# Conv front of a two-layer decoder trunk: zero fills issued early and apart, bias row added by VectorE, own replica buffers, first loads re-ordered

## The chip, the cores and the metric

The kernel runs on one core of one Trainium2 chip. The metric is the device time of one execution in microseconds (us). A run measures the kernel before and the changed kernel on the same chip; the time given of the kernel before is the median of three runs.

## What is computed

A decoder trunk of two layers over 512 tokens of width 1024, all in float32. Layer 0 is a Conformer convolution module and a mixture of experts, layer 1 is a sliding-window attention and a mixture of experts. The change is in the convolution module, in the residual sums, and in two transfers that serve the first mixture of experts.

```python
def conformer_conv(x, w1, b1, dw, dwb, g, bn, w2, b2):
    h = x @ w1 + b1                                  # (512, 2048)
    a, gate = jnp.split(h, 2, axis=-1)
    h = a * jax.nn.sigmoid(gate)
    h = lax.conv_general_dilated(                    # causal, 31 taps, each of 1024 channels alone
        h, dw[:, None, :].astype(h.dtype), window_strides=(1,),
        padding=[(CONV_WIDTH - 1, 0)], dimension_numbers=('NWC', 'WIO', 'NWC'),
        feature_group_count=D_MODEL) + dwb
    h = jax.nn.silu(layer_norm(h, g, bn))
    return h @ w2 + b2

def deepnorm(x, sub, g, b):
    return layer_norm(DEEPNORM_ALPHA * x + sub, g, b)

# layer 0: x = deepnorm(x, conformer_conv(x, ...), ...); x = deepnorm(x, grouped_moe(x, ...), ...)
# layer 1: x = deepnorm(x, swa_sink_attention(x, ...), ...); x = deepnorm(x, grouped_moe(x, ...), ...)
```

The mixture of experts sends each token to two of 16 experts. The kernel puts the tokens into a table in HBM, `xs_dram`, which has places for 512 tokens of each expert and must hold zeros where no token stands.

## The kernel before

Every engine has a program of its own, written by hand, and the engines meet at semaphores only. The names that matter here are those of the convolution front, the first 290 us.

**Input.** ScalarE (ACT) issues the loads of x in four tiles of 128 tokens (L1212), then the small parameter rows (`prm`), the convolution weights `dw_r` of 31 rows by 1024 columns (L1217), the positions, and eight small pieces of the convolution weights in another layout (`dw_a`, L1223). SyncE (SP) issues at the same time the ten loads of the first weight matrix (`conv_in`, L385; pieces 0 and 1 are one column tile of 128 channels, the others two) and two of the second (L393). TensorE (PE) transposes x (L475), VectorE (DVE) copies the result to `xT` (L823).

**Eight column tiles.** For each tile c of 128 channels TensorE makes the product for `a` and `gate` (L508); after tile 0 come some transposes of parameters (L490 to L496). ACT makes the sigmoid (L1253), and VectorE the gated product `glu(c)` into `hpad` (L841). The 31 taps of tiles 0 to 3 are done by VectorE, one instruction each (`taps(c, glus)`, L849 to L862); the table `glus` says before which tap a `glu` of a later tile stands. Tiles 4 to 7 are done by TensorE (L522) as 32 products of 32 output channels each with weights `wdw`, which GpSimd (POOL) builds in one instruction (L1496). These products read `shifted(c)`: 16 pieces of `hpad`, shifted by 0 to 3 columns, which SP copies from SBUF to SBUF with 16 DMAs a tile (`replicate(c)`, L415). The copies of tiles 4, 5 and 6 go to ring slots 1, 2 and 3, those of tile 7 to slot 1 again, and wait for TensorE to be through with tile 4 (`s_pec`). ACT moves each result out of PSUM (L1260).

**Residual.** The layer norm that follows needs `ALPHA * x + b2`. POOL makes it in place in `x_sb`, two instructions for each of four tiles (L1491, L1492), once the row `resrow` and the other rows are there (`s_rows`); VectorE adds the product of the second matrix (L900). In layer 1 POOL does the same (`residual(t)`, L1598 and L1599), and VectorE adds at L1142.

**Zero fill.** `clear_rows(i)` (L1246) writes zeros over one half of `xs_dram`, 16 MB in one DMA that ACT issues. Half 0 is issued behind the row loads in `later_loads`, half 1 after the four results of L1260. The first scatter of tokens (L1530, POOL) waits for both.

**Then.** Normalisation, second matrix (L550), router and scatter, four token tiles in a row; after that the experts, whose weights go through a ring of eight buffers. SP issues the first five of these weight loads when TensorE has done tile 7 (`s_pec` at 4).

Of the kernel before, what the change touches and what calls it, by code (L numbers as in the profile page):

```python
# [24 lines left out]
ALU = mybir.AluOpType  # L25
# [3 lines left out]
P = 128  # L29
# [50 lines left out]
def trunk(nc, x_in, positions, conv_w1, conv_b1, conv_dw, conv_dwb, conv_ln_g, conv_ln_b,  # L80
# [12 lines left out]
    with ExitStack() as ctx:  # L93
# [3 lines left out]
        def sem(name):  # L97
            return ctx.enter_context(nc.semaphore(name))
# [141 lines left out]
        s_xa = sem("s_xa")  # L240
# [119 lines left out]
        def shifted(c):  # L360

            slot_of = (1, 2, 3, 1)[c - DVE_TILES]
            return wring[:, slot_of, 0:SHIFTS * REPW].rearrange("p (g n) -> p g n", g=SHIFTS)
# [16 lines left out]
        def _(sp):  # L380
# [7 lines left out]
            conv_in(0, 1)  # L388
            conv_in(1, 1)
# [20 lines left out]
            def replicate(c):  # L410

                sp.wait_ge(s_glu, c + 1)
                for s in range(SHIFTS):
                    for q in range(SHIFTS):
                        sp.dma_start(shifted(c)[s * GRP:(s + 1) * GRP, q, :],  # L415
                                     hpad[q * GRP:(q + 1) * GRP, c, s:s + REPW]).then_inc(s_rep[c - DVE_TILES], 16)

            replicate(4)
            replicate(5)
            sp.wait_ge(s_g1, KD)  # L420
            replicate(6)
            sp.wait_ge(s_pec, 1)
            replicate(7)
# [44 lines left out]
        def _(pe):  # L468
# [18 lines left out]
            def parameters():  # L487

                pe.wait_ge(s_small, 16 * 6)
                pe.transpose(ps[:, 5, 0:NPRM], prm[:, :], ident[0:NPRM, 0:NPRM])  # L490
                for c in range(DVE_TILES):
                    pe.transpose(ps[:, 4, 32 * c:32 * c + CW], dw_r[:, c * P:(c + 1) * P], ident[0:CW, 0:CW])
                pe.wait_ge(s_dwload, 16 * ROUNDS)
                pe.transpose(ps[:, 5, P:2 * P], dw_a.rearrange("p s c -> p (s c)"), ident[:, :])
                pe.wait_ge(s_rope, 1)
                pe.transpose(ps[:, 5, 64:64 + T], pos_f[:, :], ident[0:T, 0:T]).then_inc(s_prT, 1)  # L496
# [20 lines left out]
            for c in range(DVE_TILES, KD):  # L517
                pe.wait_ge(s_glu, c + 1)
                pe.wait_ge(s_rep[c - DVE_TILES], 16 * SHIFTS * SHIFTS)
                for r in range(ROUNDS):  # L520
                    for q in range(SHIFTS):
                        last = pe.matmul(ps[q * GRP:(q + 1) * GRP, 2 * (c % 4), :],  # L522
                                         wdw[:, r, SHIFTS * (c - DVE_TILES) + q, :],
                                         shifted(c)[:, q, SHIFTS * r:SHIFTS * r + S],
                                         start=(r == 0), stop=(r == ROUNDS - 1))
                last.then_inc(s_pec, 1)
# [280 lines left out]
        def _(dve):  # L807
# [18 lines left out]

            dve.wait_ge(s_prT, 1)
# [38 lines left out]
            taps(1, {4: 2, 22: 3})  # L866
            taps(2, {7: 4, 26: 5})
            taps(3, {10: 6, 28: 7})
# [28 lines left out]
            def add_product(t, bank, signal, count):  # L897

                for h in range(2):
                    ins = dve.tensor_tensor(x_sb[:, t, h * 512:(h + 1) * 512], x_sb[:, t, h * 512:(h + 1) * 512],  # L900
                                            ps[:, bank + h, :], ALU.add)
                ins.then_inc(signal, 1)
                dve.wait_ge(signal, count)
# [77 lines left out]
            dve.wait_ge(s_rows, 16 * 8)  # L981
# [5 lines left out]
            for t in range(T):  # L987
                if t >= 2:
                    places(0, t - 2, 7)
                dve.wait_ge(s_C, t + 1)  # L990
                dve.wait_ge(s_xa, t + 1)
                add_product(t, 4, s_cadd, t + 1)
                norm_x(t, n, 0, 0)
                n += 1
                if t + 2 < T:
                    norm_conv(t + 2, n)
                    n += 1
                if t >= 1:
                    route(0, t - 1)
# [109 lines left out]
            def take(u, n):  # L1109
# [28 lines left out]
                elif kind in ("W0", "W1"):  # L1138
# [3 lines left out]
                    dve.tensor_tensor(half_x, half_x, ps[:, bank, :], ALU.add).then_inc(bank_read[bank - 5], 1)  # L1142
# [61 lines left out]
        def _(act):  # L1204
# [12 lines left out]
            act.dma_start(dw_r[:, :], conv_dw[0]).then_inc(s_small, 16)  # L1217
# [3 lines left out]
            for r in range(ROUNDS):  # L1221
# [3 lines left out]
                              ).then_inc(s_dwload, 16)  # L1225

# [4 lines left out]
            def later_loads():  # L1231
# [4 lines left out]
                act.dma_start(resrow, conv_b2[0].partition_broadcast(P)).then_inc(s_rows, 16)  # L1236
# [12 lines left out]
            for c in range(KD):  # L1249
# [5 lines left out]
                if c == 0:  # L1255
                    later_loads()

# [5 lines left out]
            clear_rows(1)  # L1263
# [183 lines left out]
        def _(pool):  # L1447
# [20 lines left out]
            pool.wait_ge(s_small, 16 * 6)  # L1468
# [18 lines left out]

            pool.wait_ge(s_x0T, T)
            pool.wait_ge(s_rows, 16 * 8)
            for t in range(T):  # L1490
                own(pool.tensor_scalar(x_sb[:, t, :], x_sb[:, t, :], ALPHA, None, ALU.mult))  # L1491
                pool.tensor_tensor(x_sb[:, t, :], x_sb[:, t, :], resrow, ALU.add).then_inc(s_xa, 1)  # L1492
# [101 lines left out]
            pool.wait_ge(s_rows1, 16 * 5)  # L1594
            def residual(t):
                full(pool, ("Xa", t))
                full(pool, ("Xb", t))
                own(pool.tensor_scalar(x_sb[:, t, :], x_sb[:, t, :], ALPHA, None, ALU.mult))  # L1598
# [41 lines left out]
```

## Time and profile before

| what | value |
|---|---|
| median of 3 runs | 1178.7 us (1175.54 to 1180.32) |
| the profiled execution, its own time | 1174.66 us |
| its span (first to last instruction) | 1173.0 us |
| mean granted TensorE clock | 0.901 of full speed |
| TensorE matmul busy | 952.7 us, 81% |
| VectorE busy | 454.5 us, 39% |
| GpSimd busy | 220.9 us, 19% |
| ScalarE busy | 169.4 us, 14% |
| DMA, mean over the span | 267 GB/s |

The table is an average over stages with different limits, so it says little on a change to one stage. The times below are read on the scale of the span; what lies around the span is 1.66 us.

### The profile page before, as it was taken

The page shows a single profiled execution, that of the slowest core. Times are in us where ns is not written, and L with a number is a line of the kernel's source. Part 1 is how long each engine was busy: PE and PEld are TensorE (multiplying, and loading weights), DVE is VectorE, ACT ScalarE, POOL GpSimd, SP SyncE. Part 2 cuts the span into 40 slices and gives each one's busy share as a digit, 9 for nine tenths or more (in the row PEclk, how much of TensorE's full clock was granted, in tenths as well). Part 3 has the DMA queues.
Part 4 walks back from the last instruction along what each step waited for, and adds up shares of the span by engine and source line. Part 5 has one row for each costly group of instructions (what it writes and reads, how often), then busy time and mean ns, then how long its engine had stood idle before and what let it go on. Part 6 is the DMA issues. An engine that isn't in the chain of part 4 may idle for free.

```text
span 1173.0 us, 13864 instructions
## 1 busy us (share of the span) xinstructions
PE 952.7 (81%) x5241; PEld 499.1 (43%) x5241; DVE 454.5 (39%) x925; ACT 169.4 (14%) x376; POOL 220.9 (19%) x314
## 2 busy tenths in 40 slices
PE   6999969983999698999379899878459977999930
PEld 3444324542555354554134454434235534555510
DVE  1799913553111011111586548564511101111126
ACT  0000021311000000001113332432020000000110
POOL 1094000024211111100431002021240212020022
PEclk8999989985999899999589999978679978999975
DMA  8994349964999999999640003201859999999932
GB/s 252 387 409 157 87 152 414 402 226 170 345 389 403 373 390 384 382 408 411 214 180 1 1 1 144 72 1 68 322 201 392 387 372 391 388 383 395 398 127 107
DMA packets 74301, 313.40 MB, mean 267 GB/s; under 512 B 8797, under 2 KB 19209, under 8 KB 57704
## 3 DMA queue, kind: packets, MB, share of 16 engines
q1 hardware_dynamic: 36752, 228.83, 51.1%
q10 hardware_dynamic: 27352, 55.35, 12.6%
q0 software_dynamic: 10112, 28.06, 6.9%
q8 instruction: 56, 0.92, 0.3%
q14 instruction: 29, 0.24, 0.1%
HBM read 252.48 MB, written 55.31 MB: 262 GB/s over the span
## 4 chain that ended last, share of the span: by engine, by line
PE 58%; DMA 18%; DVE 15%; issue 4%; ACT 2%; POOL 2%; SPq 1%; POOLq 0%; ACTq 0%; DVEq 0%
PE ps L605 20%; PE ps L615 10%; DMA wring<-in_moe_w_gate_dram 8%; DVE arena L859 7%; PE ps L711 7%; PE ps L550 5%; PE ps L730 5%; DMA wring<-in_moe_w_up_dram 3%; PE ps L508 3%; DMA arena<-in_moe_w_up_dram 2%; DMA wring<-in_conv_w_dram 1%; PE ps L756 1%; PE ps L768 1%; DMA xs_dram<-x_sb,place_i 1%; PE ps L782 1%
## 5 line engine op out<-in xcount | busy, mean ns | idle before, releaser
L605 PE MATMUL ps<-wring,arena 128*64 128x256 f32 x2016 | 246.6, 403 | 55.3 <-DVE arena L1011 28.2
L605 PEld LDWEIGHTS ps<-wring,arena 128*64 128x64 f32 x2016 | 152.0, 146 | 149.6 <-issue 56.4
L1536 POOL DMA_DIRECT2D arena<-xs_dram x172 | 91.4, 536 | 357.0 <-DVE arena L1011 336.1
L615 PE MATMUL ps<-wring,arena 128*64 128x512 f32 x560 | 126.7, 594 | 6.2 <-DVE arena L1046 5.7
L508 PE MATMUL ps<-arena,wring 128*128 128x512 f32 x256 | 113.0, 604 | 4.2 <-DMA wring<-in_conv_w_dram 4.2
L1032 DVE COPY arena<-ps 128x256 f32<-128x256 f32 x32 | 13.6, 424 | 251.3 <-PE ps L648 251.3
L859 DVE SCALAR_TENSOR_TENSOR arena<-arena,dwT 128x512 f32<-128x512 f32 x116 | 96.1, 901 | 0.0
L711 PE MATMUL ps<-wring,arena 128*128 128x512 f32 x192 | 86.3, 605 | 3.5 <-ACT arena L1384 2.7
L605 PE MATMUL ps<-arena 128*64 128x256 f32 x736 | 83.2, 380 | 0.8 <-DMA arena<-in_moe_w_up_dram 0.7
L508 PEld LDWEIGHTS ps<-arena,wring 128*128 128x128 f32 x256 | 49.5, 194 | 66.3 <-issue 66.3
L1522 POOL TENSOR_TENSOR rstd<-vareps,half 128x1 f32<-128x1 f32 x20 | 25.7, 1287 | 271.6 <-DVE vareps L875 265.9
L615 PEld LDWEIGHTS ps<-wring,arena 128*64 128x64 f32 x560 | 39.4, 137 | 71.6 <-issue 60.5
L605 PEld LDWEIGHTS ps<-arena 128*64 128x64 f32 x736 | 52.1, 137 | 32.5 <-issue 6.0
L550 PE MATMUL ps<-wring,arena 128*128 128x512 f32 x128 | 62.5, 647 | 1.9 <-ACT arena L1273 1.3
L730 PE MATMUL ps<-wring,arena 128*128 128x512 f32 x128 | 60.2, 626 | 0.0
L1011 DVE STREAM_TRANSPOSE arena<-arena 128x512 f32<-128x512 f32 x43 | 47.5, 1105 | 30.3 <-DMA arena<-xs_dram 23.4
L711 PEld LDWEIGHTS ps<-wring,arena 128*128 128x128 f32 x192 | 36.5, 194 | 46.7 <-issue 45.6
L1320 ACT ACTIVATE arena<-ps 128x512 f32<-128x512 f32 x32 | 19.1, 597 | 227.3 <-PE ps L615 227.3
L1026 DVE TENSOR_TENSOR arena<-arena,ps 128x256 f32<-128x256 f32 x32 | 13.5, 421 | 89.2 <-PE ps L605 89.2
L550 PEld LDWEIGHTS ps<-wring,arena 128*128 128x128 f32 x128 | 26.2, 210 | 33.5 <-issue 31.8
L1044 DVE TENSOR_TENSOR arena<-arena,ps 128x256 f32<-128x256 f32 x11 | 4.6, 421 | 90.0 <-PE ps L605 90.0
L730 PEld LDWEIGHTS ps<-wring,arena 128*128 128x128 f32 x128 | 25.3, 203 | 30.3 <-issue 30.3
(189 smaller groups left out, 884.6 us busy)
## 6 DMA issues: line engine op xcount, KB each, us to landing
wring<-in_moe_w_gate_dram SPq DMA_DIRECT2D x24, 2048.0 KB, 25.1
wring<-in_moe_w_up_dram SPq DMA_DIRECT2D x24, 2048.0 KB, 19.7
wring<-in_moe_w_down_dram SPq DMA_DIRECT2D x24, 2048.0 KB, 20.2
xs_dram<-zero ACTq DMA_DIRECT2D x2, 16384.0 KB, 65.1
arena<-in_moe_w_up_dram SPq DMA_DIRECT2D x8, 2048.0 KB, 27.9
arena<-in_moe_w_down_dram SPq DMA_DIRECT2D x8, 2048.0 KB, 20.3
arena<-in_moe_w_gate_dram SPq DMA_DIRECT2D x8, 2048.0 KB, 25.7
arena<-xs_dram POOLq DMA_DIRECT2D x172, 64.0 KB, 7.1
```

What stands on the lines that cost most here:

```text
L508: last = pe.matmul(ps[:, 2 * (c % 4) + h, :], w[:, k, h, (c % 2) * P:(c % 2) * P + P], xT[:, k, :], start=(k == 0), stop=(k == KD - 1))
L550: last = pe.matmul(ps[:, 4 + h, :], hc[t % 2][:, c, :], slot(4 + c // 4, 4)[:, c % 4, h * 512:(h + 1) * 512], start=(c == 0), stop=(c == K ...
L605: mm = pe.matmul(ps[h * CAP:(h + 1) * CAP, bank, 0:256], act[:, k, :], w[:, k, h * 256:(h + 1) * 256], start=(k == 0), stop=(k == KD - 1))
L615: mm = pe.matmul(ps[h * CAP:(h + 1) * CAP, bank, :], act[:, j % 2, (j // 2) * CAP:(j // 2 + 1) * CAP], w[:, j, h * 512:(h + 1) * 512], sta ...
L711: last = pe.matmul(ps[:, bank, :], xTt[:, k, :], slot(at, KD)[:, k, :], start=(k == 0), stop=(k == KD - 1))
L730: last = pe.matmul(ps[:, bank, :], oT[t % 2][:, k, :], slot(3 + h, KD)[:, k, :], start=(k == 0), stop=(k == KD - 1))
L859: dve.scalar_tensor_tensor(out=acc, in0=hpad[:, c, k:k + S], scalar=dwT[:, c, k:k + 1], in1=acc, op0=ALU.mult, op1=ALU.add).then_inc(s_tap, 1)
L1011: return dve.transpose(xgT[i].rearrange("p k (h c) -> p h k c", h=2), xg[i].rearrange("p h (c k) -> p h k c", k=KD))
L1032: dve.tensor_copy(hT[b].rearrange("p a b -> p (a b)"), ps[:, 3, 0:256]).then_inc(s_hTc, 1)
L1320: act.activation(ysb[b], ps[:, 4, :], ACT.Copy).then_inc(s_yc, 1)
L1522: pool.tensor_tensor(rstd[:, n:n + 1], vareps[:, n:n + 1], half[:, :], ALU.pow).then_inc(s_rs, 1)
L1536: pool.dma_start(where[q * QROWS:(q + 1) * QROWS, :, :], xs_tiles[q, :, bass.ds(n, 1), :, :]).then_inc(signal, 16)
```

## The change

The second zero fill is issued by ACT after the sigmoid of tile 5, and not after the last convolution result. The bias row is loaded right behind the small pieces, and VectorE adds `b2 / ALPHA` to x before it copies the parameters; the factor ALPHA goes into the instruction that adds the product (`scalar_tensor_tensor` for `tensor_tensor`). The four copies' buffers no longer overlap (`FIT` is 7 pieces to a ring slot), so the copies wait for `glu` alone, and 8 of the 16 DMAs of tile 7 are issued by ACT. SP waits for the last tile of x before it loads weight piece 1. `dw_r` is loaded in two parts, 16 and 15 rows, of 512 columns. The places of the `glu`s among the taps are new. In layer 1 POOL scales the bias row once, and no longer the four tiles.

```diff
-        def shifted(c):
-            slot_of = (1, 2, 3, 1)[c - DVE_TILES]
-            return wring[:, slot_of, 0:SHIFTS * REPW].rearrange("p (g n) -> p g n", g=SHIFTS)
+        FIT = KD * F // REPW
+        def shifted(c, q):
+            slot_of, at = divmod(SHIFTS * (c - DVE_TILES) + q, FIT)
+            return wring[:, 1 + slot_of, at * REPW:(at + 1) * REPW]
+        def replicate(eng, c, shifts):
+            eng.wait_ge(s_glu, c + 1)
+            for s in shifts:
+                for q in range(SHIFTS):
+                    eng.dma_start(shifted(c, q)[s * GRP:(s + 1) * GRP, :],
+                                  hpad[q * GRP:(q + 1) * GRP, c, s:s + REPW]).then_inc(s_rep[c - DVE_TILES], 16)
...
             conv_in(0, 1)
+            sp.wait_ge(s_x[T - 1], 16)
             conv_in(1, 1)
...
-            replicate(4)
-            replicate(5)
-            sp.wait_ge(s_g1, KD)
-            replicate(6)
-            sp.wait_ge(s_pec, 1)
-            replicate(7)
+            for c in range(DVE_TILES, KD):
+                replicate(sp, c, (0, 1) if c == KD - 1 else (0, 1, 2, 3))
...
+            dve.wait_ge(s_b2, 16)
+            own(dve.tensor_scalar(resrow, resrow, 1.0 / ALPHA, None, ALU.mult))
+            for t in range(T):
+                ins = dve.tensor_tensor(x_sb[:, t, :], x_sb[:, t, :], resrow, ALU.add)
+            own(ins)
+
             dve.wait_ge(s_prT, 1)
...
             taps(0, {18: 1})
-            taps(1, {4: 2, 22: 3})
-            taps(2, {7: 4, 26: 5})
-            taps(3, {10: 6, 28: 7})
+            taps(1, {8: 2, 28: 3})
+            taps(2, {15: 4})
+            taps(3, {5: 5, 26: 6})
+            glu(7)
...
-                    ins = dve.tensor_tensor(x_sb[:, t, h * 512:(h + 1) * 512], x_sb[:, t, h * 512:(h + 1) * 512],
-                                            ps[:, bank + h, :], ALU.add)
+                    half_x = x_sb[:, t, h * 512:(h + 1) * 512]
+                    ins = dve.scalar_tensor_tensor(out=half_x, in0=half_x, scalar=ALPHA, in1=ps[:, bank + h, :],
+                                                   op0=ALU.mult, op1=ALU.add)
...
-            act.dma_start(dw_r[:, :], conv_dw[0]).then_inc(s_small, 16)
+            taken_cols = slice(0, P * DVE_TILES)
+            act.dma_start(dw_r[0:16, taken_cols], conv_dw[0, 0:16, taken_cols]).then_inc(s_small, 16)
+            act.dma_start(dw_r[16:CW, taken_cols], conv_dw[0, 16:CW, taken_cols]).then_inc(s_small, 16)
...
+            act.dma_start(resrow, conv_b2[0].partition_broadcast(P)).then_inc(s_b2, 16)
...
-                act.dma_start(resrow, conv_b2[0].partition_broadcast(P)).then_inc(s_rows, 16)
...
                 if c == 0:
                     later_loads()
+                if c == 5:
+                    clear_rows(1)
+                if c == KD - 1:
+                    replicate(act, c, (2, 3))
...
-            clear_rows(1)
             act.wait_ge(s_rope, 2)
...
-            pool.wait_ge(s_x0T, T)
-            pool.wait_ge(s_rows, 16 * 8)
-            for t in range(T):
-                own(pool.tensor_scalar(x_sb[:, t, :], x_sb[:, t, :], ALPHA, None, ALU.mult))
-                pool.tensor_tensor(x_sb[:, t, :], x_sb[:, t, :], resrow, ALU.add).then_inc(s_xa, 1)
...
             pool.wait_ge(s_rows1, 16 * 5)
+            own(pool.tensor_scalar(resrow, resrow, 1.0 / ALPHA, None, ALU.mult))
+
             def residual(t):
                 full(pool, ("Xa", t))
                 full(pool, ("Xb", t))
-                own(pool.tensor_scalar(x_sb[:, t, :], x_sb[:, t, :], ALPHA, None, ALU.mult))
                 pool.tensor_tensor(x_sb[:, t, :], x_sb[:, t, :], resrow, ALU.add).then_inc(s_xb, 1)
```

ScalarE, from the second sigmoid to the first use of the sine table, before. L1253 is the sigmoid, L1260 moves a convolution result out of PSUM, and `xs_dram<-zero` is the fill.

```order
L1253 ACTIVATE arena<-ps,prmT 128x512 x7
L1260 ACTIVATE arena<-ps,prmT 128x512 x4
L1246 DMA xs_dram<-zero 8192x1x512
L1265 ACT_TABLE_LOAD
L1265 ACTIVATE rows<-rows 128x128
```

The same stretch of ScalarE in the changed kernel, where the sigmoid is L1262 and the move out of PSUM L1273:

```order
L1262 ACTIVATE arena<-ps,prmT 128x512 x5
L1255 DMA xs_dram<-zero 8192x1x512
L1262 ACTIVATE arena<-ps,prmT 128x512 x2
L372 DMA wring<-arena 32x540 x8
L1273 ACTIVATE arena<-ps,prmT 128x512 x4
L1277 ACT_TABLE_LOAD
L1277 ACTIVATE rows<-rows 128x128
```

The fill moved from behind the four moves to ahead of the last two sigmoids, and eight of the copies of tile 7 now stand behind it on the same engine, ahead of the four moves.

VectorE, from the copies of the transposed x to the second `glu`, before:

```order
L823 COPY arena<-ps 128x4x128 x8
L828 COPY prmT<-ps 128x40
L829 COPY posT<-ps 128x4
L830 COPY arena<-ps 128x128
L832 TENSOR_REDUCE arena<-ident 128x32
L833 COPY dwT<-ps 128x4x31
L841 SCALAR_TENSOR_TENSOR arena<-ps,prmT,arena 128x512
```

The same stretch in the changed kernel, where `glu` is L846:

```order
L822 COPY arena<-ps 128x4x128 x8
L827 TENSOR_SCALAR rows<-rows 128x1024
L829 TENSOR_TENSOR x_sb<-x_sb,rows 128x1024 x4
L833 COPY prmT<-ps 128x40
L834 COPY posT<-ps 128x4
L835 COPY arena<-ps 128x128
L837 TENSOR_REDUCE arena<-ident 128x32
L838 COPY dwT<-ps 128x4x31
L846 SCALAR_TENSOR_TENSOR arena<-ps,prmT,arena 128x512
```

Five instructions came in ahead of the parameter copies, and they wait for the bias row.

## Rows read from the trace of the kernel before

**Rows 1.** Chain of waits, first 260 us: start, duration, what; some pieces.

```profile
...
1.65 16.39 DMA wring<-in_conv_w_dram
...
18.18 16.65 PE ps L508 x32
...
144.39 0.51 SPq L415
...
155.38 1.93 DMA wring<-arena
...
```

**Rows 2.** Timeline of TensorE: start, duration, line, what, count, [idle before <-releaser].

```profile
...
10.83 3.17 PE L475 MATMUL ps<-ident,x_sb 128*128 128x128 f32 x16 [0.17 <-DMA x_sb<-in_x_dram]
...
35.71 96.40 PE L508 MATMUL ps<-arena,wring 128*128 128x512 f32 x224
132.04 20.81 PE L522 MATMUL ps<-wring 128*32 128x512 f32 x192
157.45 8.37 PE L522 MATMUL ps<-wring 128*32 128x512 f32 x64 [4.60 <-DMA wring<-arena]
...
236.39 16.77 PE L550 MATMUL ps<-wring,arena 128*128 128x512 f32 x32
...
284.92 12.98 PE L605 MATMUL ps<-wring,arena 128*64 128x256 f32 x96 [11.51 <-DVE arena L1011]
...
```

**Rows 3.** Timeline of VectorE, same columns.

```profile
...
67.74 26.79 DVE L859 SCALAR_TENSOR_TENSOR arena<-arena,dwT 128x512 f32<-128x512 f32 x18
...
107.56 12.66 DVE L859 SCALAR_TENSOR_TENSOR arena<-arena,dwT 128x512 f32<-128x512 f32 x19
...
124.83 0.54 DVE L849 TENSOR_SCALAR arena<-arena,dwT,prmT 128x512 f32<-128x512 f32 x1
...
146.33 0.69 DVE L862 TENSOR_TENSOR arena<-arena 128x512 f32<-128x512 f32 x1
...
244.92 1.28 DVE L894 SCALAR_TENSOR_TENSOR x_sb<-x_sb,rstd,lnrow 128x1024 f32<-128x1024 f32 x1 [8.52 <-POOL rstd L1522]
...
```

**Rows 4.** Timeline of VectorE, narrow window around 84 us.

```profile
...
84.17 7.57 DVE L859 SCALAR_TENSOR_TENSOR arena<-arena,dwT 128x512 f32<-128x512 f32 x1
```

**Rows 5.** Timeline of GpSimd.

```profile
...
65.15 3.19 POOL L1491 TENSOR_SCALAR x_sb<-x_sb 128x1024 f32<-128x1024 f32 x1
68.43 2.91 POOL L1492 TENSOR_TENSOR x_sb<-x_sb,rows 128x1024 f32<-128x1024 f32 x1
...
83.67 7.53 POOL L1496 TENSOR_TENSOR wring<-arena 128x4096 f32<-128x4096 f32 x1
...
241.70 1.25 POOL L1530 DMA_INDIRECT xs_dram<-x_sb,place_i  x1 [23.30 <-DMA xs_dram<-zero]
...
```

**Rows 6.** Timeline of ScalarE.

```profile
...
104.68 0.69 ACT L1253 ACTIVATE arena<-ps,prmT 128x512 f32<-128x512 f32 x1 [13.05 <-PE ps L508]
...
```

**Rows 7.** Windows: engines' busy us, clock, DMA share, GB/s.

```profile
...
80.00:90.00 10.00, 10.00 (x25) 4.48 (x24) 10.00 (x5) 0.00 (x0) 9.92 (x3) 1.00 1.05 410
...
110.00:120.00 10.00, 10.00 (x25) 4.44 (x24) 10.00 (x16) 0.69 (x1) 0.00 (x0) 1.00 0.41 97
...
```

**Rows 8.** DMA issues, first 260 us: KB each, median us to landing.

```profile
...
rows<-in_conv_b_dram ACTq DMA_DIRECT2D x1, 512.0 KB, 6.8
...
sinkb<-in_attn_sinks_dram ACTq DMA_DIRECT2D x1, 8.0 KB, 14.0
```

**Rows 9.** Instructions of line L1246, the fills.

```profile
...
DMA to landing us min/median/max: 54.6/65.1/75.5
```

**Rows 10.** Instructions of line L415: duration ns min, median, max; landing.

```profile
...
L415 SPq DMA_DIRECT2D wring<-arena x64: 507/591/1769, 107.7 to 155.4; - x64
...
DMA to landing us min/median/max: 1.9/2.0/3.3
```

**Rows 11.** Instructions on x_sb, 560 to 740 us: duration ns min, median, max.

```profile
...
L1079 DVE TENSOR_TENSOR x_sb<-x_sb,arena x4: 1224/1224/1226, 570.6 to 592.3; 128x1024 f32<-128x1024 f32 x4
L1598 POOL TENSOR_SCALAR x_sb<-x_sb x3: 2771/2774/2793, 597.0 to 713.5; 128x1024 f32<-128x1024 f32 x3
...
```

More of the change, by code:

```diff
@@ L239, in trunk @@
         s_pecv = sem("s_pecv")
-        s_xa = sem("s_xa")
+        s_b2 = sem("s_b2")
         s_At = sem("s_At")
@@ L408, in consumed @@
                 sp.wait_ge(s_dn if kind == 2 else s_gud, E * l + e + 1)
[L410 to L416, printed above, removed]
-            replicate(4)
-            replicate(5)
-            sp.wait_ge(s_g1, KD)
-            replicate(6)
-            sp.wait_ge(s_pec, 1)
-            replicate(7)
+            for c in range(DVE_TILES, KD):
+                replicate(sp, c, (0, 1) if c == KD - 1 else (0, 1, 2, 3))
             sp.wait_ge(s_pec, KD - DVE_TILES)
@@ L487, in parameters @@
             def parameters():
-                pe.wait_ge(s_small, 16 * 6)
+                pe.wait_ge(s_small, 16 * 7)
                 pe.transpose(ps[:, 5, 0:NPRM], prm[:, :], ident[0:NPRM, 0:NPRM])
@@ L523, in _ @@
                                          wdw[:, r, SHIFTS * (c - DVE_TILES) + q, :],
-                                         shifted(c)[:, q, SHIFTS * r:SHIFTS * r + S],
+                                         shifted(c, q)[:, SHIFTS * r:SHIFTS * r + S],
                                          start=(r == 0), stop=(r == ROUNDS - 1))
@@ L978, in table @@
                                   ALU.mult)
-            dve.wait_ge(s_rows, 16 * 8)
+            dve.wait_ge(s_rows, 16 * 7)
             n = 0
@@ L990, in _ @@
                 dve.wait_ge(s_C, t + 1)
-                dve.wait_ge(s_xa, t + 1)
                 add_product(t, 4, s_cadd, t + 1)
@@ L1141, in take @@
                     half_x = x_sb[:, t, h * 512:(h + 1) * 512]
-                    dve.tensor_tensor(half_x, half_x, ps[:, bank, :], ALU.add).then_inc(bank_read[bank - 5], 1)
+                    dve.scalar_tensor_tensor(out=half_x, in0=half_x, scalar=ALPHA, in1=ps[:, bank, :],
+                                             op0=ALU.mult, op1=ALU.add).then_inc(bank_read[bank - 5], 1)
                     if h == 1 and t == T - 1:
@@ L1467, in _ @@
             pool.memset(hpad[:, :, 0:CW - 1], 0.0).then_inc(s_pool0, 1)
-            pool.wait_ge(s_small, 16 * 6)
+            pool.wait_ge(s_small, 16 * 7)
             pool.tensor_copy(pos_f[:, :], pos_i[:, :]).then_inc(s_rope, 1)
```

## The prediction

> **What bounds the kernel now.** The chain of waits comes first, because an average over 1173 us hides a front of 166. It begins with a DMA: TensorE's first product waits until the first weight piece has landed at 18.04 us (1.65 + 16.39), and tile 0 then takes 16.65 us [rows 1]. The timeline of TensorE shows what follows: the other seven tiles in one piece of 96.40 us, 13.77 a tile, then the convolution products of tiles 4, 5 and 6 in one piece of 20.81 us, 6.94 each, and only then a hole: tile 7 starts at 157.45 and not at 152.85, and takes 8.37 us [rows 2]. The reader is to see that TensorE never waits for VectorE between 18 and 152 us; it pays for VectorE's delay once, at tile 7. The chain of waits says how: SP issues the copies of tile 7 from 144.39, when `glu(7)` is done, the last one at about 155, and it lands 1.93 us later [rows 1]. From the end of tile 7 (165.82) to the first expert product (284.92) are 119.1 us of work in sequence on four token tiles [rows 2].
>
> Why `glu(7)` is late stands in the timeline of VectorE. Undisturbed, 19 taps take 12.66 us, 0.667 each; but from 67.74 us 18 taps take 26.79 us, 14.8 more than 12.0 [rows 3]. One tap of these lasts 7.57 us [rows 4]. GpSimd's table tells why: the instruction L1496 starts at 83.67 and lasts 7.53 us, and ahead of it stand the residual instructions of 3.19 and 2.91 us [rows 5]. A tap that meets one of them waits until it ends. So of the 14.8 us some 6.9 (7.57 less 0.667) belong to L1496, and 7.9 to the residual pass, which began still earlier.
>
> The Trainium skill, "SBUF — State Buffer", section "Who interferes with whom", says that VectorE and GpSimd share one port pair as an exclusive lock held for a whole instruction. By that rule the trace agrees: 7.57 beside 7.53 us.
>
> **The change, part by part.** *First loads.* Before, pieces 0 and 1 of the weights and x came together. Now piece 0 (1 MB) and x (2.1 MB) come alone. Lower bound of the gain: if x lands no sooner, its transposes still end at 14.0 (10.83 + 3.17) [rows 2] and VectorE's last copy some 1.3 us later, so the products start at 15.4, a gain of 2.8. Upper bound: 3.1 MB at the best rate of the trace, 410 GB/s [rows 7], from 1.65 us, is 9.2 us; with one tile of transposes and copies, about 2.0 + 1.3, the start is at 12.6, a gain of 5.5. I take 4.5, near the upper end, since also the one load of 31 rows is replaced by two smaller ones: start at 13.7. The whole TensorE row moves with it: tile 5 ends at 100.2 instead of 104.7 [rows 6], and tile 7's convolution could start at 148.35 instead of 152.85.
>
> *Bias row on VectorE.* Four additions of 1.224 us [rows 11] and one scaling of the row, twice the 0.54 us of half its width [rows 3]: 6.0 us. They stand where VectorE waits for the transposed parameters, which come after tile 0, at about 31 us. The row is issued at about 11 us; such a load took 6.8 us to land [rows 8]. 18 + 6 = 24 leaves 7 us. The cover is gone if the row lands after 25; each us later then moves the taps by one, and not yet TensorE, which asks for these copies only at tile 2, 14 us later. Cost 0.
>
> *Residual pass off GpSimd.* VectorE gains at least the 7.9 us of the stretch shown. L1496 stays; it now waits for tile 1 only and costs its 7 us earlier. With 4.5 from the start and 7.9, the taps end by 134 instead of 147.0 [rows 3], `glu(6)`, five taps, the sum and one `glu` ahead of that, by 129.5, `glu(7)` by 135. The copies of a tile cost SP 16 issues, from 144.39 to 155.3 = 10.9 us [rows 1] with one slow issue, and 0.59 + 0.04 otherwise, 10.1; they land in 2.0 us [rows 10]. Tile 6: 129.5 + 10.1 + 2.0 = 141.6, and TensorE is through with tile 5 at 141.4. So tiles 4 to 6 are in time. With own buffers nothing else holds them. SP's half of tile 7: 139.6 + 5.1 + 2.0 = 146.7, before 148.35.
>
> *ACT's half of tile 7, and the fill.* This is the step on which the sum rests. ACT issues the second fill at 100.9 (the sigmoid of tile 5 starts 4.5 us ahead of 104.68 and lasts 0.69 [rows 6]). It is 16.8 MB, at 410 GB/s 41 us; with about 1 us to its first packet it would end at 142.9 alone. SP puts 40 copies of 69 KB beside it meanwhile. Their cost to the fill: by bytes 2.8 MB at 410 GB/s, 6.8 us; by their share of the DMA engines alone, 0.41 [rows 7] over the 25 us of their issue, 10 us. I take 8.3: end at 151.2. The eight copies which ACT issues at 130 to 140 stand in ACT's own queue behind the fill. That a queue keeps its order is what the row of `sinkb` shows: a load of 8 KB, issued behind 2.6 MB in the same queue, took 14.0 us to land [rows 8], where a copy from a queue that is empty took 2.0 [rows 10]. So the eight copies land at 151.2 + 1.7 (0.55 MB, between 1.3 and 2.3) + 2.0 = 154.9, 6.5 us after TensorE is ready. Bounds: 152.5 to 157 with the two costs above. TensorE idles as it did before and runs tile 7 as slowly as then, 8.37 us: end at 163.3 instead of 165.8. **Front: 2.5 us gained** (0.4 to 4.9). Queued behind those DMAs on ACT are the four moves out of PSUM; even if ACT is held at the issue until the fill has drained, they (0.69 each) are done within tile 7.
>
> The Trainium skill, "DMA: Bandwidth & Descriptors", section "Queues, rings and completion order", says that on each DMA engine the descriptors of one queue are consumed in ring order. By that rule the sum is 2.5 us; without it, it would be the 10.5 of the first rival.
>
> *Fill away from 166 to 241 us.* Before, it took 75.5 us to land [rows 9] beside the expert weights, and GpSimd waited 23.3 us for it at the first scatter [rows 5]; VectorE stood 8.5 us for the square root queued behind [rows 3]. TensorE had 16.77 us of products in hand then, from 236.39 to 253.2 [rows 2], and VectorE was back before they ended. The stall is hidden; worth 0. The experts' first weights are there long before 284.92 in either case.
>
> *ALPHA in the adding instruction.* Same width, one operand more; no difference above 0.1 us each.
>
> *Layer 1.* GpSimd scales the bias row (1024 columns, as long as the 2.77 us of the tile scaling it replaces [rows 11]) at the same point, so the collision with VectorE there stays. Three later scalings fall away, beside TensorE's products. Worth 0 to 2, I take 0.3.
>
> Sum: 1174.66 − 2.5 − 0.3 = 1171.9 for the profiled execution, whose own time is 4.0 us below the median of 1178.7. On the scale of the median: **1176**.
>
> **The rivals.** *The fill is through in time* (its interference is near nothing, or ACT's copies pass it). Then tile 7 starts at 148.35 and, without a hole, takes 6.94: end at 155.3, gain 10.5, with layer 1 10.8: **1168**. Against it speaks that even an undisturbed fill ends at 142.9 and its copies at 146.6, so that only 1.7 us of disturbance may be added where 6.8 is the smaller estimate; for it, that ACT's DMAs may start on engines that finish early. Chance 0.22.
>
> *The fill is slow beside the copies* (the slower side). Beside other loads the fill before took 75.5 us [rows 9]. If ours ends at T, the front ends at T + 3.7 + 8.4; it is worse than before from T = 153.7, and by 6 us from T = 160, a fill of 59 us instead of 50. At T = 162 the time is **1187**. For it: DMAs among SBUF rows use 0.41 of the engines for 97 GB/s, so they are dear; against it: they are few. Chance 0.15.
>
> *The re-ordering of the loads does nothing*, because piece 0 lands late for another reason, the many small rows in ACT's queue: start gain 0 to 1, everything after moves back 4 us, the fill too: **1180**. Against it: these small loads are issued from 7 us on, after piece 0. Chance 0.13.
>
> **How the numbers follow.** The forecast as worked has 0.50. What a measurement of this kernel tells from no change is 0.5%, 5.9 us. Faster by more: the first rival, and the forecast's upper edge (an earlier start and a fill end at 149), 0.22 + 0.12 = 0.34. Slower by more: most of the second rival, a little of the third, 0.15. Within: 0.51. The forecast's own range is 1171 to 1180; reaching to the first rival and to half of the second it is 1166 to 1183.
>
> **What would show it.** Right: TensorE's first L508 product near 13.7 us; no tap longer than 0.8 us but the one beside GpSimd's long instruction, now near 46 us; the fill issued near 101 and landed near 151 to 153; ACT's eight copies landing after it, and TensorE idle before tile 7's convolution for 4 to 9 us. Wrong: tile 7 following tile 6 at once (first rival); a fill longer than 58 us (second); a first product after 17 us (third); or a first `glu` later than 35 us, which would mean that the bias row holds VectorE.

## The result, and the profile after

The changed kernel takes 1191.99 us (median of four runs, 1190.86 to 1192.97), the kernel before 1177.12 on the same chip: ratio 1.0111, 95% interval 1.0076 to 1.0145. It is slower by 1.1%. The forecast of 1176 and its range, 1166 to 1183, missed it.

The timeline of TensorE of the changed kernel, in the columns of [rows 2], says where:

```profile
...
13.15 1.97 PE L474 MATMUL ps<-ident,x_sb 128*128 128x128 f32 x8 [0.18 <-DMA x_sb<-in_x_dram]
16.50 16.03 PE L507 MATMUL ps<-arena,wring 128*128 128x512 f32 x32 [1.38 <-DVE arena L822]
...
33.40 96.40 PE L507 MATMUL ps<-arena,wring 128*128 128x512 f32 x224
129.73 7.07 PE L521 MATMUL ps<-wring 128*32 128x512 f32 x64
147.99 9.90 PE L521 MATMUL ps<-wring 128*32 128x512 f32 x64 [11.19 <-DMA wring<-arena]
163.09 16.05 PE L521 MATMUL ps<-wring 128*32 128x512 f32 x128 [5.20 <-DMA wring<-arena]
...
297.02 12.28 PE L604 MATMUL ps<-wring,arena 128*64 128x256 f32 x96 [11.56 <-DVE arena L1017]
...
```

The products start 1.7 us earlier than before, and the eight tiles run in one piece as they did. Then there are two holes where there was one, of 11.19 us ahead of tile 5's convolution and of 5.20 us ahead of tile 6's; tile 7's follows tile 6's at once. Tile 7 ends at 179.1 us and not at 165.8 [rows 2], and the first expert product stands at 297.02 instead of 284.92, 12.1 us later. The spans of the two profiled executions differ by 16.8 us; the other 4.7 come behind this point and are looked at below.

VectorE is not to blame. Its timeline in the changed kernel:

```profile
...
16.72 1.71 DVE L827 TENSOR_SCALAR rows<-rows 128x1024 f32<-128x1024 f32 x1 [0.28 <-DMA rows<-in_conv_b_dram]
18.46 4.63 DVE L829 TENSOR_TENSOR x_sb<-x_sb,rows 128x1024 f32<-128x1024 f32 x4
33.59 0.20 DVE L833 COPY prmT<-ps 128x40 f32<-128x40 f32 x1 [10.49 <-PE ps L495]
...
111.38 0.75 DVE L846 SCALAR_TENSOR_TENSOR arena<-ps,prmT,arena 128x512 f32<-128x512 f32 x1
...
125.95 0.76 DVE L846 SCALAR_TENSOR_TENSOR arena<-ps,prmT,arena 128x512 f32<-128x512 f32 x1
...
130.66 0.74 DVE L846 SCALAR_TENSOR_TENSOR arena<-ps,prmT,arena 128x512 f32<-128x512 f32 x1
...
```

The bias row and its additions (L827, L829) are over at 23.1 us, 10.49 us before the parameter copies can start. `glu(5)`, `glu(6)` and `glu(7)` (L846) stand at 111.4, 126.0 and 130.7; before, `glu(7)` ended at 144.3. The DMAs are late. This is the chain of waits of the changed kernel around the second fill, which ACT issues at 102.38 us; SPq is SP at the issue of a copy:

```profile
...
101.78 0.59 SPq L372
...
103.04 0.85 SPq L372
...
103.94 1.53 SPq L372
...
152.98 2.56 SPq L372
155.58 0.86 SPq L372
156.47 0.59 SPq L372
...
160.91 2.04 DMA wring<-arena
...
163.09 16.09 PE ps L521 x128
...
```

An issue takes 0.59 us until the fill begins, 1.4 to 2.6 us while it runs, and 0.59 again from 156.47 on. ACT's own issue of the fill lasted 0.59 us and was over at 103.0, so the long issues on SP are not two engines issuing at one time. The counts of the copies' line (duration of an issue in ns: least, median, most), beside [rows 10], and the landing by issuing engine:

```profile
...
L372 SPq DMA_DIRECT2D wring<-arena x56: 588/1410/2557, 97.3 to 166.0; - x56
L372 ACTq DMA_DIRECT2D wring<-arena x8: 633/1652/15897, 131.4 to 157.4; - x8
...
```

```profile
...
xs_dram<-zero ACTq DMA_DIRECT2D x2, 16384.0 KB, 53.7
...
wring<-arena SPq DMA_DIRECT2D x56, 67.5 KB, 6.4
...
wring<-arena ACTq DMA_DIRECT2D x8, 67.5 KB, 5.6
...
```

The median issue on SP went from 0.591 to 1.410 us, the median landing from 2.0 to 6.4. One issue on ACT took 15.9 us: the first one behind the fill. The fill itself landed 54.3 us after its issue, at 156.7; at its old place it took 75.5 [rows 9]. The windows show both transfers sharing what there is; the columns are those of [rows 7]:

```profile
...
110.00:120.00 10.00, 10.00 (x25) 4.46 (x24) 10.00 (x17) 0.69 (x1) 0.00 (x0) 1.00 1.03 366
...
130.00:140.00 10.00, 6.81 (x64) 1.82 (x56) 1.37 (x3) 0.53 (x1) 0.00 (x0) 1.00 1.03 365
140.00:150.00 10.00, 2.01 (x12) 0.69 (x16) 0.00 (x0) 0.00 (x0) 0.00 (x0) 0.50 1.03 366
...
```

The DMA engines are full (1.03), at 366 GB/s in place of the 410 of [rows 7] with the first fill alone under way. From 103.94 to 152.98 us SP issues 28 copies of 69 KB, one each 1.75 us: 39 GB/s of that, where the copies alone reached 97 GB/s [rows 7].

The holes have a second price. In the window from 140 to 150 us, the first 8 us of which are hole, the granted clock (third number from the end) is 0.50, which is TensorE's lower level, 1.2 GHz. Tile 5's products behind the hole ran at a mean of 0.71 and took 9.90 us, where tile 4's took 7.07 at 1.00.

### The profile page after: what moved, and what is told of

Same layout as the page of the kernel before. It is cut to its first block, busy times and chain, and to the rows that moved or that the text cites. A ratio compares the mean times of both kernels' runs of the same rounds, so it can differ in the third digit from the quotient of the medians.

```text
span 1189.8 us, 13853 instructions
## 1 busy us (share of the span) xinstructions
PE 959.9 (81%) x5241; PEld 501.7 (42%) x5241; DVE 446.8 (38%) x930; ACT 169.5 (14%) x376; POOL 188.3 (16%) x303
## 4 chain that ended last, share of the span: by engine, by line
PE 44%; DMA 18%; issue 17%; DVE 11%; SPq 5%; POOL 3%; ACT 1%; ACTq 0%; POOLq 0%; DVEq 0%
PE ps L604 20%; DMA wring<-in_moe_w_gate_dram 11%; PE ps L614 9%; SPq L372 5%; PE ps L549 5%; DVE arena L864 3%; PE ps L507 3%; DMA arena<-in_moe_w_up_dram 2%; PE ps L729 2%; POOL rstd L1528 1%; PE ps L521 1%; DMA xs_dram<-x_sb,place_i 1%; PE ps L474 1%; DMA x_sb<-in_x_dram 1%; DVE bns L878 1%
## 5 line engine op out<-in xcount | busy, mean ns | idle before, releaser
L614 PE MATMUL ps<-wring,arena 128*64 128x512 f32 x560 | 126.7, 594 | 6.2 <-DVE arena L1052 5.7
L864 DVE SCALAR_TENSOR_TENSOR arena<-arena,dwT 128x512 f32<-128x512 f32 x116 | 84.3, 802 | 0.0
L710 PEld LDWEIGHTS ps<-wring,arena 128*128 128x128 f32 x192 | 37.9, 202 | 49.4 <-issue 48.3
L521 PE MATMUL ps<-wring 128*32 128x512 f32 x256 | 33.0, 678 | 16.4 <-DMA wring<-arena 16.4
L549 PEld LDWEIGHTS ps<-wring,arena 128*128 128x128 f32 x128 | 25.8, 207 | 32.9 <-issue 31.3
```

The costliest lines, as they stand in the source:

```text
L549: last = pe.matmul(ps[:, 4 + h, :], hc[t % 2][:, c, :], slot(4 + c // 4, 4)[:, c % 4, h * 512:(h + 1) * 512], start=(c == 0), stop=(c == K ...
L614: mm = pe.matmul(ps[h * CAP:(h + 1) * CAP, bank, :], act[:, j % 2, (j // 2) * CAP:(j // 2 + 1) * CAP], w[:, j, h * 512:(h + 1) * 512], sta ...
L710: last = pe.matmul(ps[:, bank, :], xTt[:, k, :], slot(at, KD)[:, k, :], start=(k == 0), stop=(k == KD - 1))
L864: dve.scalar_tensor_tensor(out=acc, in0=hpad[:, c, k:k + S], scalar=dwT[:, c, k:k + 1], in1=acc, op0=ALU.mult, op1=ALU.add).then_inc(s_tap, 1)
```

## Experiments

Theory A: the early fill and the copies share the DMA engines, and what suffers is the issue and landing of the copies, which TensorE waits for. Theory B: the copies are slow or late for another reason that came with the change (two issuing engines, the buffers, ACT held at its issue). The total is measured over several runs of a kernel, the rows come from one profiled execution of it. All ratios are to the kernel before on the same chip.

**Late fill.** The changed kernel, with one line back at its old place.

```diff
-                if c == 5:
-                    clear_rows(1)
...
+            clear_rows(1)
             act.wait_ge(s_rope, 2)
```

> The changed kernel with the second zero fill issued where it was before, after the four moves of L1260. Theory A (the early fill shares the DMA engines with the copies of hpad and stretches their issue on SP from 0.59 to 1.4 us each, so tiles 5 to 7 of the convolution wait): copies back at 0.59 to 0.63 us, tile 7 follows tile 6 with no hole, front ends near 157 us instead of 179, first expert product near 276 instead of 297, total 1168 to 1172. Theory B (the copies are slow for another reason, such as two engines issuing them or the new places of their buffers): copies stay above 1 us, the holes before tiles 5 and 6 stay, total 1185 or more.

Measured: 1165.79 us, ratio 0.9876 (0.9831 to 0.9921). Its timeline of TensorE:

```profile
...
16.59 14.00 PE L507 MATMUL ps<-arena,wring 128*128 128x512 f32 x32 [1.38 <-DVE arena L822]
...
127.80 27.68 PE L521 MATMUL ps<-wring 128*32 128x512 f32 x256
...
272.99 13.10 PE L604 MATMUL ps<-wring,arena 128*64 128x256 f32 x96 [11.59 <-DVE arena L1017]
...
```

and its copies:

```profile
...
L372 SPq DMA_DIRECT2D wring<-arena x56: 507/591/1597, 95.4 to 140.4; - x56
...
DMA to landing us min/median/max: 1.9/2.0/3.8
```

All four convolution products run in one piece of 27.68 us; no hole is left. The issue is back at 0.591 us, the landing at 2.0. The first expert product is 24.0 us earlier than in the changed kernel. Of these, 1.9 us stand already where the convolution products start (127.80 and 129.73), because tile 0's products took 14.00 us here and 16.03 there; the same group took 15.66 and 15.90 us in two other runs with a late fill, so this part varies between executions. The fill's place costs the other 22 us: holes of 16.4 and slower products behind them (9.90 + 16.05 us for tiles 5 to 7, where all four tiles take 27.68 without a hole).

Theory B falls for the two issuing engines and the new buffers: both are still in this kernel. ACT is no longer held at its issue, so this run alone doesn't exclude that.

**Only the early fill.** The kernel before, and nothing but the fill moved.

```diff
                 if c == 0:
                     later_loads()
+                if c == 5:
+                    clear_rows(1)
...
-            clear_rows(1)
             act.wait_ge(s_rope, 2)
```

> The kernel before, with this one part of the change alone: the second fill issued after the sigmoid of tile 5. Theory A: the 64 copies on SP take 1.4 us each while the fill runs (about 105 to 158 us), some 37 are done by then, the rest take 0.63 us, so the last lands near 178 us and the front ends near 186 instead of 166: total 1190 to 1198. Theory B: copies stay at 0.59 us, total within 4 us of the kernel before.

Measured: 1205.47 us, ratio 1.0191 (1.0150 to 1.0233), more than expected. Its timeline of TensorE:

```profile
...
139.45 9.77 PE L522 MATMUL ps<-wring 128*32 128x512 f32 x64 [7.69 <-DMA wring<-arena]
159.82 9.82 PE L522 MATMUL ps<-wring 128*32 128x512 f32 x64 [10.61 <-DMA wring<-arena]
169.95 7.07 PE L522 MATMUL ps<-wring 128*32 128x512 f32 x64 [0.31 <-DMA wring<-arena]
181.60 9.18 PE L522 MATMUL ps<-wring 128*32 128x512 f32 x64 [4.57 <-DMA wring<-arena]
...
308.63 12.31 PE L605 MATMUL ps<-wring,arena 128*64 128x256 f32 x96 [11.54 <-DVE arena L1011]
...
```

Four holes of 7.69, 10.61, 0.31 and 4.57 us, and the first expert product 23.7 us later than before. The eight tiles' products had ended at the same time (131.8 and 132.1), so all of it is the fill's: some 24 us in the old kernel, 22 in the new one. The expectation was too low, largely because it took 1.4 us for an issue, the changed kernel's median, which mixes issues inside and outside the fill; inside, a copy goes out each 1.76 us here. And ACT issues no copies in this kernel, so the last form of theory B falls too: the holes need neither a second issuing engine, nor the new buffers, nor an ACT that is held.

**Fill behind ACT's copies.** The changed kernel, with `clear_rows(1)` moved from tile 5 to right behind `replicate(act, c, (2, 3))`.

```diff
-                if c == 5:
-                    clear_rows(1)
                 if c == KD - 1:
                     replicate(act, c, (2, 3))
+                    clear_rows(1)
```

> The changed kernel with the second fill issued by ACT behind its eight copies of tile 7, near 137 us. Theory A: only the last copies of tile 6 and of SP's half of tile 7 could meet it; the front ends near 158, and the fill is over before the expert weights need the engines: total within 3 us of the run with the late fill. Theory B: as slow as the changed kernel, since nothing but the fill's place is changed, 1185 or more.

Measured: 1174.94 us, ratio 0.9945 (0.9920 to 0.9971), slower than the late fill by about 0.7%, some 8 us, where at most 3 were expected.

```profile
...
126.47 20.81 PE L521 MATMUL ps<-wring 128*32 128x512 f32 x192
151.72 8.77 PE L521 MATMUL ps<-wring 128*32 128x512 f32 x64 [4.45 <-DMA wring<-arena]
...
278.01 12.69 PE L604 MATMUL ps<-wring,arena 128*64 128x256 f32 x96 [11.58 <-DVE arena L1017]
...
```

The fill now starts at 134.8 us, when SP still has tile 7's half to issue; its last eight copies meet it, the last of them takes 8.57 us to land, and a hole of 4.45 us stands ahead of tile 7. The size was misjudged, the kind was right: eight copies in the fill are enough for a hole.

**Half of the fill early.** The changed kernel, 8 MB after the sigmoid of tile 5 and 8 MB at the old place.

```diff
-                act.dma_start(xs_halves[i], zero[:, :].unsqueeze(1).to_broadcast([P, E * S // P, 512])).then_inc(s_xinit, 16)
+                part = (slice(0, 64), slice(0, 32), slice(32, 64))[i]
+                act.dma_start(xs_halves[min(i, 1)][:, part, :], zero[:, :].unsqueeze(1).to_broadcast([P, part.stop - part.start, 512])).then_inc(s_xinit, 16)
...
+            clear_rows(2)
             act.wait_ge(s_rope, 2)
...
-                    pool.wait_ge(s_xinit, 32)
+                    pool.wait_ge(s_xinit, 48)
```

> The changed kernel with only half of the second fill (8 MB) issued after the sigmoid of tile 5, the other half after the four moves as before. Theory A: the copies are slow only until about 128 us; tile 5's 16 copies take some 19 us, tile 6's and 7's 10 us again, and no hole stays ahead of tiles 5 to 7, or one under 2 us; front ends near 157, total 1166 to 1170. Theory B (the place of the fill matters by itself, as with ACT being held at its issue): the holes stay.

Measured: 1174.03 us, ratio 0.9924 (0.9892 to 0.9957), slower than the 1166 to 1170 expected.

```profile
...
127.22 13.94 PE L521 MATMUL ps<-wring 128*32 128x512 f32 x128
144.17 15.64 PE L521 MATMUL ps<-wring 128*32 128x512 f32 x128 [3.01 <-DMA wring<-arena]
...
277.73 12.32 PE L604 MATMUL ps<-wring,arena 128*64 128x256 f32 x96 [11.56 <-DVE arena L1017]
...
```

With half the bytes one hole of 3.01 us is left, ahead of tile 6, where the whole fill made 16.4 in two. The delay grows faster than the bytes. A likely reason, not tested alone, is that the first copies that are slowed have slack, since tile 4's and most of tile 5's are issued well before TensorE asks for them.

**Fill in shorter rows.** The changed kernel, the second fill in rows of 1 KB, same bytes.

```diff
-                act.dma_start(xs_halves[i], zero[:, :].unsqueeze(1).to_broadcast([P, E * S // P, 512])).then_inc(s_xinit, 16)
+                d = 512 if i == 0 else 256
+                rows_of = xs_dram.rearrange("(i p n) (h d) -> i p (n h) d", i=2, p=P, d=d)[i]
+                act.dma_start(rows_of, zero[:, 0:d].unsqueeze(1).to_broadcast([P, E * S // 2 // P * D // d, d])).then_inc(s_xinit, 16)
```

> The changed kernel, its early second fill cut into rows of 1 KB instead of 2 KB, with the same bytes. Theory A1 (on each DMA engine the copies and the fill take turns row by row, so a copy waits for fill rows): with shorter fill rows the copies' issue gets shorter than 1.55 us, near 1.0, the fill longer, and the front ends earlier than 179 us. Theory A2 (the making of the fill's descriptors is what holds the copies): twice as many descriptors, issue near 2.5 us, front ends after 190. Theory A3 (shared by bytes): issue stays near 1.5 us.

Measured, in a single run: 1194.47 us.

```profile
...
L372 SPq DMA_DIRECT2D wring<-arena x56: 590/1476/2114, 95.0 to 166.0; - x56
...
DMA to landing us min/median/max: 2.0/6.0/29.3
```

```profile
...
144.99 8.71 PE L521 MATMUL ps<-wring 128*32 128x512 f32 x64 [10.54 <-DMA wring<-arena]
164.86 15.88 PE L521 MATMUL ps<-wring 128*32 128x512 f32 x128 [11.16 <-DMA wring<-arena]
...
```

The median issue is 1.476 us beside 1.410: neither 1.0 nor 2.5. Inside the fill a copy goes out each 1.73 us, beside 1.75. Twice as many rows of half the size leave the pace of the copies as it was, so it is not the count of the fill's rows that sets it. The fill itself does get longer, 59.7 us to landing beside 54.3, with 340 GB/s moved from 110 to 120 us where it was 366. So 33 copies are issued inside it instead of 29, and the holes add up to 21.7 us instead of 16.4. Of the three theories the one on bytes fits the pace; how the engines divide their time between the two stays open.

**Residual back on GpSimd.** The run with the late fill, and layer 0's residual pass as before, with all that belongs to it: the plain addition on VectorE, and the load of the bias row at its old place.

```diff
-            dve.wait_ge(s_b2, 16)
-            own(dve.tensor_scalar(resrow, resrow, 1.0 / ALPHA, None, ALU.mult))
-            for t in range(T):
-                ins = dve.tensor_tensor(x_sb[:, t, :], x_sb[:, t, :], resrow, ALU.add)
-            own(ins)
...
+            for t in range(T):
+                own(pool.tensor_scalar(x_sb[:, t, :], x_sb[:, t, :], ALPHA, None, ALU.mult))
+                pool.tensor_tensor(x_sb[:, t, :], x_sb[:, t, :], resrow, ALU.add).then_inc(s_xa, 1)
```

> The run with the late fill, with the residual pass of layer 0 back on GpSimd as in the kernel before. It should cost VectorE 12 us of blocked taps again; the new places of the glus and own buffers stay. glu(7) near 140 us instead of 130, glu(6) near 135; the copies of tile 6 then land near 147 us, those of tile 7 near 154, and TensorE waits 4 to 8 us: total 5 to 9 us above the late fill's. Rival: the gain is in the own buffers and the second issuing engine alone; total equal.

Measured: 1180.09 us, ratio 0.9997 (0.9966 to 1.0028), against 0.9895 for the late fill on the same chip.

```profile
...
127.69 13.94 PE L521 MATMUL ps<-wring 128*32 128x512 f32 x128
148.60 16.86 PE L521 MATMUL ps<-wring 128*32 128x512 f32 x128 [6.97 <-DMA wring<-arena]
...
282.97 12.87 PE L604 MATMUL ps<-wring,arena 128*64 128x256 f32 x96 [11.58 <-DVE arena L1011]
...
```

The hole of 6.97 us is back, and the first expert product is 10.0 us later than with the late fill. `glu(7)` starts at 140.5 us instead of 128.7. The whole gain of that version rests on this edit; without it, it equals the kernel before within the interval. The new places of the `glu`s among the taps are in both, and were not undone alone.

**Parts that show no effect.** Three more runs each undo one part of the version with the late fill: the wait of SP for x, ACT's half of the copies, the own buffers.

```diff
-            sp.wait_ge(s_x[T - 1], 16)
```

> The run with the late fill, and SP no longer waits for the last tile of x before it loads weight piece 1. If the wait is worth what the two traces differ by (first product at 16.5 instead of 18.2 us), the first product starts near 18 us and the total is 1 to 2 us above the late fill's. Rival: the gain came from the two smaller loads of dw_r, and the wait is worth nothing: start near 16.5, total equal.

```diff
-                if c == KD - 1:
-                    replicate(act, c, (2, 3))
...
-                replicate(sp, c, (0, 1) if c == KD - 1 else (0, 1, 2, 3))
+                replicate(sp, c, (0, 1, 2, 3))
```

> The run with the late fill, all 64 copies issued by SP. SP is through with tile 6 near 133 to 136 us; 16 more issues end at 146 and land at 148, and TensorE is ready for tile 7 near 148.5. If each issue costs 0.63 us, no hole or one under 1 us: total equal to the late fill's within 2 us. Rival: ACT's half was needed, a hole of several us ahead of tile 7, total 3 to 6 us more.

```diff
-            slot_of, at = divmod(SHIFTS * (c - DVE_TILES) + q, FIT)
-            return wring[:, 1 + slot_of, at * REPW:(at + 1) * REPW]
+            slot_of = (1, 2, 3, 1)[c - DVE_TILES]
+            return wring[:, slot_of, q * REPW:(q + 1) * REPW]
...
             eng.wait_ge(s_glu, c + 1)
+            if c == 6:
+                eng.wait_ge(s_g1, KD)
+            if c == 7:
+                eng.wait_ge(s_pec, 1)
```

> The run with the late fill, with the buffers and the waits of the copies as in the kernel before (tile 6 waits for all eight products, tile 7 for the convolution of tile 4). Tile 6's copies then start at 127.8 instead of 123 and land at 140, TensorE asks for them at 141.5; tile 7's start at 138 on SP and at 135 on ACT and land at 145, asked for at 148.5. Own buffers would be worth nothing: total equal within 2 us. Rival: they were the gain, a hole ahead of tile 6 or 7 of 4 us or more.

Measured: ratios 0.9902 (0.9865 to 0.9939), 0.9894 (0.9825 to 0.9962) and 0.9894 (0.9824 to 0.9964), beside 0.9876 (0.9831 to 0.9921) and, repeated, 0.9895 (0.9856 to 0.9935) for the version with all of them. The intervals can't tell the five apart; each reaches some 4 to 8 us to either side, so an effect of 1 or 2 us on the total would not be seen. The first products and the start of tile 7's convolution say the same:

```profile
...
15.54 14.00 PE L506 MATMUL ps<-arena,wring 128*128 128x512 f32 x32 [1.69 <-DVE arena L821]
...
```

```profile
...
150.79 7.07 PE L521 MATMUL ps<-wring 128*32 128x512 f32 x64 [0.23 <-DMA wring<-arena]
...
```

Without the wait for x the products start at 15.54 us, no later than with it (16.59, and 15.39 in the repeated run). With SP alone the hole is 0.23 us. With the old buffers (third run) the four products are one piece again, of 27.67 us.

**Layer 1 as before.** The late fill, and layer 1's residual as in the kernel before, with VectorE's plain addition.

```diff
-            own(pool.tensor_scalar(resrow, resrow, 1.0 / ALPHA, None, ALU.mult))
-
             def residual(t):
                 full(pool, ("Xa", t))
                 full(pool, ("Xb", t))
+                own(pool.tensor_scalar(x_sb[:, t, :], x_sb[:, t, :], ALPHA, None, ALU.mult))
```

> The run with the late fill, with layer 1's residual as in the kernel before (GpSimd scales each tile by ALPHA, VectorE adds plainly). Predicted worth 0 to 2 us: total 0 to 2 us above the late fill's. Rival: the changed kernel's 4 us more between the first expert product and the end came from this edit; then this run is 3 to 5 us faster than the late fill's.

Measured: 1168.28 us, ratio 0.9884 (0.9847 to 0.9921): no difference. The 4.7 us behind the first expert product are something else. In the attention TensorE starts a group of products after a short wait; two such groups in the changed kernel, and then the windows over them:

```profile
...
628.33 8.72 PE L710 MATMUL ps<-wring,arena 128*128 128x512 f32 x16 [0.89 <-ACT arena L1396]
...
669.16 8.79 PE L710 MATMUL ps<-wring,arena 128*128 128x512 f32 x16 [0.88 <-ACT arena L1396]
...
```

```profile
...
628.00:637.00 9.00, 8.67 (x18) 3.61 (x18) 1.04 (x3) 3.11 (x11) 1.94 (x1) 0.80 0.01 2
668.00:678.00 10.00, 9.12 (x20) 3.72 (x20) 2.88 (x8) 2.83 (x11) 0.00 (x0) 0.77 0.01 2
...
```

Before, the same two groups took 7.10 and 7.11 us at a granted clock of 1.00; here the mean is 0.80 and 0.77, so part of each ran at the lower level, 1.2 GHz. But the run with layer 1 as before has groups of 9.13 and 9.02 us too. And so has the run that is the kernel before with only the fill moved:

```profile
...
639.71 8.87 PE L711 MATMUL ps<-wring,arena 128*128 128x512 f32 x16 [0.89 <-ACT arena L1385]
...
```

From the first expert product to the end the profiled executions range from 888.1 us (kernel before) to 898.9 (layer 1 as before), with the version of the late fill at 891.1 and 894.5, and the kernel before with the early fill at 896.2, though nothing behind the fill differs there from the 888.1. So it follows none of the edits of the convolution front or of layer 1. What sets it wasn't found; the kernel before was profiled in an execution at the low end of it (1174.66 us beside medians of 1177 to 1182).

**Late fill, repeated.**

> The run with the late fill once more, in five rounds. It should be 1.0 to 1.4% under the kernel before.

Measured: 1167.39 us (six runs), ratio 0.9895 (0.9856 to 0.9935). The version with the late fill beats both kernels, by 1.0 to 1.2% the one before and by some 2% the changed one.

## Why the prediction was wrong

**The step that failed** is in the part on ACT's half of tile 7 and the fill, and in the sentence ahead of it that tiles 4 to 6 are in time. The fill's interference was charged to the fill alone, with two estimates of what SP's copies take from it. What the fill takes from the copies was left out: their issue was kept at 0.59 + 0.04 us and their landing at 2.0 through the whole fill. The runs showed an issue each 1.75 us inside the fill, and 6.4 us to landing. Tile 5's copies landed at 148, when TensorE had asked for them since 137, and tile 6's at 163 instead of 141.6. The price of this was 22 us, the largest term of all, and it was not in the sum. The rows gave a sign of it: the fill alone takes 1.05 of the DMA engines and the copies alone 0.41 [rows 7], 1.46 together, so one of the two had to give way, and the prediction let only the fill do so. Even with both slowed alike the estimate would have fallen short, at 0.63 x 1.46 = 0.92 us for a copy where 1.75 were measured. That SP's issue itself gets longer stands in no row, though the trace of the kernel before has long issues too: the ten weight loads of L385, among the other first loads, took SP 3.0 us each at the median.

**The fill's own time** was fairly judged: 41 us and 8.3 of interference were expected, 54.3 in all were measured. The slower rival was built on that length, and gives no account of the 1192 either. Its formula (T + 3.7 + 8.4) with the measured T = 156.7 puts the end of the front at 168.8, 3 us later than before; it ended at 179.1. And its wait stands ahead of tile 7, where TensorE did not wait at all.

**The copies in ACT's queue behind the fill** behaved as forecast: the first was held for 15.9 us at its issue and landed at 155.6, the last at 160.2, around the fill's end at 156.7. It cost nothing here, since TensorE asked for tile 7's copies only at 171 us. The Trainium skill's rule on ring order in "DMA: Bandwidth & Descriptors", section "Queues, rings and completion order", agrees with the 24.2 us from that first copy's issue to its landing, and was on a part that turned out off the path. The same page, section "Issuing engines are not separate DMA queues", says that DMAs of all issuing engines run on the same 16 DMA engines and interleave. That is the rule that bears on this case, and the trace agrees: SP's copies landed in the middle of ACT's fill, 6.4 us after their issue at the median of all 56.

**First loads**: sized too high. The start was put at 13.7 and came at 16.5, a gain of 1.7 instead of 4.5, and below the lower bound of 2.8. That bound took the transposes of x to end at 14.0 as before; the last tile of x landed at 13.10 us, far from the 9.2 of the upper bound, and they ended at 15.1. The start varies between executions: it lies at 15.25 to 16.87 us in the eleven profiled ones with the two smaller loads of `dw_r`, and at 18.18 and 18.99 in the two with the one large load. The gain isn't the wait's: without it the start was at 15.54. Nor does it need the bias row's new place: the run with the residual back on GpSimd loads that row where it was before, and starts at 16.48. By elimination the two smaller loads of `dw_r` remain as its cause; they were not undone alone.

**Bias row on VectorE**: right. Cost 0, with 10.49 us of room left where 7 were expected.

**Residual pass off GpSimd**: right, and the source of all the gain there is. `glu(6)` ended at 126.7 and `glu(7)` at 131.4, where 129.5 and 135 were given as limits. The instruction that was L1496 still blocked one tap, which took 6.3 us from 48.9 on. (Of the sum for the taps: 147.0 less 4.5 and 7.9 is 134.6, not 134; they ended at 130.7.)

**Fill away from 166 to 241 us, ALPHA, layer 1**: no effect shows, as predicted. From the end of tile 7 to the first expert product it is 119.1 us before, 117.9 with the fill early and 117.5 with the late fill and the other edits. The adding instruction takes 0.682 us with ALPHA and without. The undoing of layer 1's part made no difference that the interval can show.

## What to carry to other kernels

A bulk transfer moved to a place where its own engine is free may land in the middle of small transfers of another queue that somebody waits for, as it did here. Price both directions: what the small ones take from the bulk, and by how much the small ones' pace and landing grow, here 2.8 (1.75 for 0.63 us) and 3.2 times. Before work is moved out of a late stretch, see that it costs something there: this fill ran hidden beside 119 us of other work, and leaving it there while keeping the rest of the change gave 1.0 to 1.2%.

## What was not expected of the hardware

SP's issue instruction itself got longer, from 0.59 to between 1.4 and 2.6 us, with another engine's DMA under way, and was back at 0.59 two issues after that ended. A single 16 MB fill held SP's copies back to 39 GB/s of the 366 that moved (40 of 340 with rows of 1 KB). The first issue on ACT behind the fill took 15.9 us (24.6 with rows of 1 KB), and ACT did nothing else meanwhile: tile 4's result was ready at 136.8 us and left PSUM only at 158.0, behind the last of the eight issues.
